# Twelve of sixteen experts' outputs take a way through memory instead of a product on TensorE

## The reference, cut to what matters

```python
for e in range(N_EXPERTS):                 # 16 experts, D_EXPERT = 512, D_MODEL = 1024
    h = jax.nn.silu(t @ w1[e]) * (t @ w3[e])
    out = out + gates[:, e:e + 1] * (h @ w2[e]).astype(jnp.float32)
```

## Time and profile before

| | |
|---|---|
| median of 3 runs | 1024.15 us (1023.99 to 1028.38) |
| the profiled execution | 1026.94 us |
| its span, first to last instruction | 1025.3 us |
| busy: PE, DVE, ACT, POOL | 949.1, 340.7, 168.0, 109.2 us |
| bytes moved by DMA | 266.96 MB |
| mean granted clock of TensorE | 0.965 |

### The profile page before, as it was taken

The page is one execution under the profiler, slowest core; times in us unless marked ns, Lnnn a source line. Parts: engine busy times, 40 slices in busy tenths (PEclk is TensorE's granted clock), DMA queues, the critical chain, the costliest instruction groups (busy, mean ns, idle before and its releaser), DMA issues.

```text
span 1025.3 us, 14418 instructions
## 1 busy us (share of the span) xinstructions
PE 949.1 (93%) x4830; PEld 486.0 (47%) x4831; DVE 340.7 (33%) x815; ACT 168.0 (16%) x337; POOL 109.2 (11%) x198
## 2 busy tenths in 40 slices
PE   6999999899989999988999999999999999999993
PEld 4666545444344444335656755554544343443331
DVE  0975454521221221225215533215512212222115
ACT  1000051111011011112214333211111110111010
POOL 0260100111001001004200033000110010110000
PEclk9999999799999999998999999999599999999997
DMA  7866584796979999969403303395496499999961
GB/s 180 234 213 203 177 336 170 297 341 255 369 299 381 378 396 392 424 252 319 131 2 89 123 22 143 125 378 200 137 330 253 167 403 383 390 398 401 401 274 52
DMA packets 74614, 266.96 MB, mean 260 GB/s; under 512 B 7528, under 2 KB 39300, under 8 KB 66353
## 3 DMA queue, kind: packets, MB, share of 16 engines
q1 hardware_dynamic: 64112, 237.74, 62.1%
q10 hardware_dynamic: 5057, 16.15, 4.5%
q0 software_dynamic: 5392, 12.34, 4.2%
HBM read 259.78 MB, written 7.15 MB: 260 GB/s over the span
## 4 chain that ended last, share of the span: by engine, by line
PE 83%; DVE 6%; DMA 6%; ACT 3%; issue 1%; SPq 0%; DVEq 0%; ACTq 0%
PE bank L1030 21%; PE bank L1038 10%; PE bank L976 5%; PE wide L1073 5%; DMA w<-in_e_w 5%; PE bank L910 4%; PE bank L799 4%; PE wide L799 3%; PE bank L815 3%; PE wide L910 3%; PE wide L1882 3%; PE bank L1744 2%; PE bank L1712 2%; PE wide L1696 2%; PE wide L1921 1%
## 5 line engine op out<-in xcount | busy, mean ns | idle before, releaser
L1030 PE MATMUL bank<-w,dbuf 128*64 128x512 f32 x960 | 216.2, 602 | 5.5 <-DMA w<-in_e_w 2.6
L1030 PEld LDWEIGHTS bank<-w,dbuf 128*64 128x64 f32 x960 | 74.9, 139 | 141.1 <-issue 141.1
L1038 PE MATMUL bank<-w,dbuf 128*64 128x512 f32 x480 | 112.4, 610 | 11.0 <-DVE dbuf L1478 11.0
L1483 DVE COPY dbuf<-bank 64x512 f32<-64x512 f32 x64 | 44.0, 688 | 156.1 <-PE bank L1038 155.7
L1474 DVE TENSOR_TENSOR dbuf<-dbuf,bank 64x512 f32<-64x512 f32 x32 | 22.1, 690 | 187.4 <-ACT dbuf L717 187.4
L717 ACT ACTIVATE dbuf<-bank 64x512 f32<-64x512 f32 x32 | 18.9, 591 | 391.0 <-PE bank L1030 391.0
L976 PEld LDWEIGHTS bank<-ident,dbuf 64*128 64x128 f32 x448 | 58.0, 219 | 38.1 <-issue 36.2
L1038 PEld LDWEIGHTS bank<-w,dbuf 128*64 128x64 f32 x480 | 37.5, 140 | 70.2 <-issue 70.2
L976 PE MATMUL bank<-ident,dbuf 64*128 64x64 f32 x448 | 65.3, 285 | 1.9 <-DVE dbuf L1474 1.7
L1073 PE MATMUL wide<-dbuf,ukT 128*128 128x512 f32 x128 | 63.0, 617 | 3.0 <-DVE dbuf L1483 3.0
L555 POOL COPY idx_col<-idx 64x1 int32 (+1 forms) x32 | 5.7, 179 | 544.8 <-PE bank L976 357.3
(11 more groups left out here) (365 smaller groups left out, 1130.2 us busy)
## 6 DMA issues: line engine op xcount, KB each, us to landing
w<-in_e_w SPq DMA_DIRECT2D x90, 2048.0 KB, 16.1
dbuf<-in_a_w_pw SPq DMA_DIRECT2D x16, 512.0 KB, 8.1
w<-u_rows SPq DMA_DIRECT2D x32, 142.0 KB, 2.9
dbuf<-in_a_w_pw ACTq DMA_DIRECT2D x4, 1024.0 KB, 6.3
dbuf<-in_e_w SPq DMA_DIRECT2D x2, 2048.0 KB, 18.0
w<-in_cache_ckv SPq DMA_DIRECT2D x32, 128.0 KB, 2.9
dbuf<-in_cache_ckv SPq DMA_DIRECT2D x32, 128.0 KB, 2.1
dbuf<-in_b_w_o SPq DMA_DIRECT2D x2, 2048.0 KB, 8.0
```

The source lines that it names most:

```text
L1030: last = nc.tensor.matmul(bank[n * C:(n + 1) * C], x[:, k], w[n][k], start=(k == 0), stop=(k == KD - 1))
L1038: last = nc.tensor.matmul(bank[n * C:(n + 1) * C], h[:, k], w[k][:, n * 512:(n + 1) * 512], start=(k == 0), stop=(k == 3))
L1483: last = V.tensor_copy(y_pair[s * C:(s + 1) * C, h * 512:(h + 1) * 512], DOWN[h * C:(h + 1) * C, :])
```

## The change

Of the 16 experts the first twelve (`FAR = 12`) no longer go through put products. When such an expert's output stands in its half of `y_pair`, ScalarE stores the 64 rows to `y_rows` in memory, at 64 e (`store_y`). VectorE waits for the store of expert e - 2 before it writes the same half again. The routing now also computes, for each token and each of its two choices, the row 64 expert + rank (`y_idx`) and the gate (`y_gate`). A choice among the last four experts, or one with a rank of 64 or more, gets the row 768, which holds zeros.

After the store of expert 11 GpSimd fetches the 2 x 320 rows with six indirect DMAs (`gather_outputs`), into `x_tok` and `y_other`. It does so between the gathers of token rows for experts 14 and 15. ScalarE multiplies the first choice by its gate (`scale_outputs`, ahead of expert 14's silu), VectorE adds the second one (`add_gated`, behind expert 14's `copy_y`), and TensorE adds the sum to the totals as a product with the identity, in expert 15 (`add_outputs`). The two last pairs, experts 12 to 15, keep their gates and put products, those of the first in expert 14 and those of the second at the end. The further rounds keep theirs in all experts. Besides, some semaphores are merged, and attention's first products wait for all three of their loads.

```diff
+    FAR = 12
+    NO_ROW = FAR * C
+    PAIRS = (E - FAR) // 2
...
+        y_rows = [nc.dram_tensor(f"y_rows{l}", [NO_ROW + 1, D], F32).ap() for l in range(DEPTH)]
+        y_gate = part(ukT_buf, 1120, 6)
+        y_other = [part(dbuf, 14080, D), part(dbuf, 15104, D), part(xT_buf, 0, D)]
+        y_idx = sb("y_idx", [P, 6], I32)
...
+            def gather_outputs():
+                for s in range(2):
+                    pool.wait_ge(y_stored[s], FAR // 2 * 16 * (l + 1))
+                for n in range(2):
+                    for i, (t0, m) in enumerate(TILES):
+                        dst = y_other[i][0:m] if n else x_tok[0:m, i]
+                        nc.gpsimd.indirect_dma_start(dst, None, y_rows[l], bass.IndirectOffsetOnAxis(
+                            ap=y_idx[0:m, 3 * n + i:3 * n + i + 1], axis=0)).then_inc(y_in, 16)
...
+            gather_next(FAR, 0)
+            gather_outputs()
+            further(FAR + 1)
+            gather_next(FAR + 1, 1)
...
+            def store_y(e, s):
+                act.wait_ge(y_copied, e + (g0 + 1))
+                act.dma_start(y_rows[l][bass.ds(e * C, C)], y_pair[s * C:(s + 1) * C]).then_inc(y_stored[s], 16)
+            def scale_outputs():
+                act.wait_ge(y_in, 96 * (l + 1))
+                for i, (t0, m) in enumerate(TILES):
+                    nc.scalar.activation(x_tok[0:m, i], x_tok[0:m, i], ACT.Copy, scale=y_gate[0:m, i:i + 1])\
+                        .then_inc(y_scaled, 1)
...
+            def add_outputs(i):
+                t0, m = TILES[i]
+                pe.wait_ge(y_summed, 3 * l + i + 1)
+                for h in range(2):
+                    nc.tensor.matmul(TOTAL[i][h], ident[0:m, 0:m], x_tok[0:m, i, h * 512:(h + 1) * 512], start=False,
+                                     stop=False)
...
+            mark(V.tensor_copy(by_token(own_slot), top_at[:, :, 0:2].rearrange("p i k -> p k i")))
+            mark(V.tensor_scalar(past6, rank6, float(C), float(E * C), ALU.is_ge, ALU.mult))
+            after(V.tensor_tensor(picked, oh, gates.unsqueeze(1).to_broadcast([P, 2, 3, E]), ALU.mult))
+            mark(V.tensor_reduce(y_gate, picked6, AX.X, ALU.add))
+            after(V.scalar_tensor_tensor(own_slot, own_slot, float(C), rank6, ALU.mult, ALU.add))
+            after(V.tensor_tensor(own_slot, own_slot, past6, ALU.add))
+            mark(V.tensor_scalar(y_idx[:], own_slot, float(NO_ROW), None, ALU.min))
...
-            build_pair(0, p0)
...
+            def add_gated():
+                for i, (t0, m) in enumerate(TILES):
+                    dve.wait_ge(y_scaled, 3 * l + i + 1)
+                    V.scalar_tensor_tensor(x_tok[0:m, i], y_other[i][0:m], y_gate[0:m, 3 + i:4 + i], x_tok[0:m, i],
+                                           ALU.mult, ALU.add).then_inc(y_summed, 1)
...
-                    pe.wait_ge(ld_kv, 32)
+                    pe.wait_ge(ld_kv, 48)
```

More of the change, by code:

```diff
@@ L751, in act_experts @@
             silu(g0 + E - 1)
-            copy_hot(E // 2 - 1 + 8 * l)
+            copy_hot(PAIRS * l + 1)
             further(E - 1)
@@ L827, in add_channels @@
                 pe.wait_ge(acc_done, 2 * j + 2)
-                last = nc.tensor.matmul(B[4][:, 0:T], ones[:], acc[:, j], start=(j == 0), stop=(j == KD - 1))
-                if j == KD - 1:
-                    last.then_inc(sum_done, 1)
+                nc.tensor.matmul(B[4][:, 0:T], ones[:], acc[:, j], start=(j == 0), stop=(j == KD - 1))
                 pe.wait_ge(sq_done, j + 1)
@@ L1112, in pe_experts, with expert @@
             n1, n0 = 16 * 8 * l, 16 * 7 * l
-            p0 = E // 2 * l
-            def expert(e, s, w, n13, n2, n_next, pair):
-                first = isinstance(e, int) and e == 0
+            p0 = PAIRS * l
+            def expert(e, s, w, n13, n2, n_next, hot=None, put_pair_of=None):
                 do_up(e + g0, s, w, n13)
@@ L1121, in expert @@
                     turn(e + (g0 + 1), 1 - s, n_next)
-                if s == 1:
-                    turn_hot(pair + p0)
-                elif first:
+                if hot is not None:
+                    turn_hot(hot, e + g0)
+                if isinstance(e, int) and e == 0:
                     pe.wait_ge(cnt_set, l + 1)
-                else:
-                    put_rows(pair + (p0 - 1), range(0, 2))
-                do_hidden(e + g0)
-                if s == 0 and not first:
-                    put_rows(pair + (p0 - 1), range(2, PUTS))
-                do_down(e + g0, s, w, n2, None if s == 0 else pair + (p0 + 1))
+                if isinstance(e, int) and e == E - 1:
+                    add_outputs(0)
+                    add_outputs(1)
+                if put_pair_of is not None:
+                    put_rows(put_pair_of, e + g0 - 1, range(0, 2))
+                do_hidden(e + g0)
+                if put_pair_of is not None:
+                    put_rows(put_pair_of, e + g0 - 1, range(2, PUTS))
+                if isinstance(e, int) and e == E - 1:
+                    add_outputs(2)
+                do_down(e + g0, s, w, n2, None if hot is None else hot + 1)
                 further(e, w)
```

136 lines of the change are left out of this document (83 added, 53 removed).

## The result

The changed kernel takes 1059.05 us (median of 4 runs, 1056.95 to 1062.71), the kernel before 1025.03 us beside it: a ratio of 1.0322, 95% interval 1.0298 to 1.0345. It is 3.2% slower; 1054 was predicted, with a range from 1036 to 1078. The profiled execution took 1056.95 us with a span of 1055.3, where 1057.1 had been worked out for the profiled execution.

A forecast was written before the change was run, and what follows sets the result against it. The weights' loads, not TensorE, were taken as the bound from expert 14 on. Layers of +12.6 and +17.6, together +30.2 us on the profiled 1026.9, gave 1057.1, as a median 1054 us, range 1036 to 1078.

The forecast's parts named there:

- a faster TensorE gains only what idle time of the DMA engines it removes: Expert stages: of 24.5 us of TensorE work removed a layer, only earlier weight loads count.
- the weights, not TensorE, set when the layer ends: From expert 14 on: weights land at 16.8 us an expert with row gathers beside them, against TensorE's 15.3.
- The DMA share: Sign in the changed profile: share at 1.0 from about expert 3 on in both layers, 5.8 MB more a layer.
- Layer 0's stream moves 7.8 us forward: After expert 5's overflow round: weight loads resume 5.7 + 4.1 - 1.95 = 7.8 us earlier.
- The stores: Twelve stores of 256 KB a layer, 0.65 us each; 4.6 us delay in layer 0, 5.9 in layer 1.
- The fetches: Six gathers a layer, 2.62 MB, ahead of expert 14's weights: 12 us, the middle of 9.3 and 13.9.
- an extra for each instruction: Gather price: 0.77 us beyond engine time for each of six instructions, on top of 9.3 us, making 13.9.
- The end of the layer: Expert 15: identity products add the fetched outputs, priced like a pair's put products at 3.84 us, once a layer.
- The clock: Expert 14's up products may start slow after TensorE waits: 2.0 us a layer, total 1058; kept in the range only.
- A: TensorE stays the bound and the removed products are gained: -20.7 us a layer, -41 us, 983 us; chance 3%.
- B: The added transfers cost nothing, but the stream is no faster: -4 us, 1020 us, within 0.5%; chance 5%.
- C: Gathered rows reach ScalarE late, before it can gate expert 14: 19 us late in each layer, 1092 us; chance 8%.
- D: Transfers disturb each other more, stores at 1.7 us and gathers at 17 us: 1081 us; chance 9%.

The follow-up runs named there:

- the run with light weights: Half of the up weights of experts 5 to 15 not loaded: the changed kernel took 1002.61 us, the kernel before, treated the same, 1033.88 us.

## Why the prediction was right

**The bound.** The steps "a faster TensorE gains only what idle time of the DMA engines it removes" and "the weights, not TensorE, set when the layer ends" held. Without stores and fetches the stretch stays as it was (131.4 and 131.6 us), with all put products kept the loss stays as it is (266.0 and 265.9), and with lighter weights the same change gains 3%. The DMA share, predicted at 1.0 from about expert 3 on, is 0.85 over 246 to 302 and 1.01 from there to 411. TensorE's waits were predicted at about 4 us ahead of each expert and 10 or more near expert 14: from expert 9 on in layer 0 they go back and forth between 0.6 and 5.4 us, with 9.30 ahead of expert 14 (8.94 in layer 1).

**The recovered idle time, mis-sized.** "Layer 0's stream moves 7.8 us forward": by the kernel without stores and fetches it moved 2.5. The mechanism needed TensorE to free the buffers 4.1 us earlier for each pair of put products. Instead it stalled for 2.85 us ahead of expert 3, where it had not stalled in layer 0 before, and a set of down products that takes 3.65 us otherwise took 5.26 at 269.82 (granted clock 0.92 over 270 to 290). The load that ends the first gap came no earlier: expert 3 starts 37.2 us after silu 0, before 36.9. Of the 8.2 us of the first two pairs 2.3 were left at the overflow round (84.1 for 86.4), and nothing in the five kernels with the longer stall (86.6 to 88.1). Why TensorE stalls there stays open.

**The stores.** Predicted 0.65 us each, measured 0.49 in layer 0, 3.4 instead of 4.6 us, and 0.74 in layer 1 of the same two kernels. The price by bytes holds within what the traces can tell.

**The fetches, priced too high.** Predicted 12 us, measured 8.3 in layer 0, between the price by bytes (6.3) and that by engine time (9.3), and 6.2 to 7.0 in layer 1 of the kernels with a second such stretch. The 1.7 us for each 64-row gather in the earlier trace rows did not scale: ten times that would be 17. That is near one of the prediction's own signs of being wrong, that 128 rows cost much less than twice 64. The step from 6.3 to 12 us was the middle of two prices, 9.3 by engine time and 13.9 with an extra for each instruction; no run shows the latter, nor an extra for index or queue. The rate over 411 to 445 fell from 417 GB/s to 378, over the whole stretch from 388 to 386.

In layer 0, then, -2.5 + 3.6 + 8.0 = +9.1 (3.6 and 8.0 from silu 0 on), where -7.8 + 4.6 + 12 = +8.8 was predicted. The close sum is in good part luck: an error of 5.3 us on what is recovered, and of 5.0 with the opposite sign on stores and fetches. In layer 1 they cancelled less, 10.6 for 13.8; its parts could not be measured one by one, since the kernels without transfers have another routing there. The total was met by luck too: the terms of the sum come to 24.2 us where 30.2 was predicted, and the rest of the 30.0 us is the clock at expert 14 (3.5), which the sum left out, and 2.2 us ahead of expert 0 that come and go between profiles.

**The end of the layer.** 3.8 us predicted for the additions, 3.1 measured, and 3.1 and 1.4 for the whole end. The eight added instructions that were predicted are twelve (L1127 x24 over both layers). In layer 1 the kernel before had a set of down products of 5.35 us in expert 15, and the changed one has 3.65, which covers most of that difference.

**The clock.** It was left out of the sum, with +2.0 us a layer held ready. It came, with 1.7 and 1.8 us. That the put products just ahead of expert 14 would keep it up was wrong: idle time of 9.30 us stands between them. With all put products kept, too, expert 14's products took 8.97 us, after 8.46 us of waiting.

**The rivals.** A and B are refuted by the experiments: neither kind of transfer is free. C did not come about. GpSimd issued the first fetch at 404.66, and ScalarE could scale the rows at 431.12, 14.6 us before it had expert 14's silu to do; its timeline:

```profile
431.12 3.22 ACT L777 ACTIVATE x_tok<-x_tok,ukT 128x1024 f32<-128x1024 f32 x3 [7.77 <-DMA xT<-y_rows,y_idx]
445.70 0.59 ACT L748 ACTIVATE dbuf<-bank 64x512 f32<-64x512 f32 x1 [11.36 <-PE bank L1075]
```

All six were there 26.5 us after the first was issued, where 46 us had been the point from which it decides. ScalarE did wait 7.77 us for them, which the prediction had named as a sign of being wrong, but in time in which it had nothing else to do. D is refuted: it wants 1.7 us a store and 17 us for the fetches, and the highest readings are 0.74 and 11.4.

## What to carry to other kernels

Work taken from an engine that waits for a stream is worth only the gaps that it closes in the stream: find them first, and then price every byte that the new way adds to the stream at the full rate. A longer wait costs twice, since the idle time also lowers TensorE's clock for what comes next (1.7 to 1.9 us at expert 14), whether the work in front of it was removed or not. And a stretch that is read from one profile is known no better than it repeats: here to some 3 us. Here the way through memory would pay only where the weights leave room, as the run with light weights shows.

## What the runs showed that was not expected

- TensorE, with less to do, stalled at places where it waits for nothing that the profile shows: 2.85 us ahead of expert 3 after the change, up to 5.20 us in the other kernels with the same program up to there, and 4.17 us in the middle of equal products once the loop was written out.
- Reading back 2.62 MB cost 7.4 to 8.4 us of a saturated stream in layer 0 and 6.2 to 7.0 in layer 1, with and without indices and from either queue, against 6.3 us by its bytes.
- Products that fill a wait to its end keep expert 14's products at 7.09 us; where 2.57 and 3.00 us of the wait remained, they took 8.78.
- Kernels with the same transfers have stretches of 142.2 to 146.3 us, and the longer ones move more bytes before expert 14's weights have landed.
